# The conditioning projection in four column tiles of TensorE, spread over attention and the dense feed-forward

## The reference, cut to what matters

```python
def _modulation(cvec, w, b):
    return (jax.nn.silu(cvec) @ w + b)[:, None, :]

def _layer(x, mod, p, cache, ffn):
    sh1, sc1, g1, sh2, sc2, g2 = jnp.split(mod, 6, axis=-1)
    y, ctx_state = _token_mixers(_rmsnorm(x, p['norm1']) * (1 + sc1) + sh1, p, cache)
    x = x + g1 * y
    x = x + g2 * ffn(_rmsnorm(x, p['norm2']) * (1 + sc2) + sh2)
```

## Time and profile before

| | us |
|---|---|
| Median of 3 runs (2623.82 to 2625.38) | 2624.83 |
| The profiled execution's own time | 2626.07 |
| Its span | 2624.3 |
| TensorE busy | 2336.5 (89%) |
| VectorE busy | 1585.4 (60%) |
| ScalarE busy | 1094.0 (42%) |
| Mean granted TensorE clock | 0.924 of full |

### The profile page before, as it was taken

The page is one execution under the profiler, slowest core; times in us unless marked ns, Lnnn a source line. Parts: engine busy times, 40 slices in busy tenths (PEclk is TensorE's granted clock), DMA queues, the critical chain, the costliest instruction groups (busy, mean ns, idle before and its releaser), DMA issues.

```text
span 2624.3 us, 52068 instructions
## 1 busy us (share of the span) xinstructions
PE 2336.5 (89%) x22774; PEld 1463.2 (56%) x22774; DVE 1585.4 (60%) x2462; ACT 1094.0 (42%) x1398; POOL 71.5 (3%) x70
## 2 busy tenths in 40 slices
PE   7799998869789999999899998868787999998894
PEld 4366667856445555555456668855563444444442
DVE  0364645549554545533174654549638999997886
ACT  0223342226432222221132342235526888886774
POOL 0000000000000000000000000000001111110001
PEclk9889988978889999999989997988878999999997
DMA  9621100010122212214821101010009999998995
GB/s 337 209 73 50 34 29 15 4 68 1 65 81 81 81 65 97 81 49 139 278 73 50 34 1 43 4 68 1 1 19 368 402 409 407 408 408 343 360 355 223
DMA packets 58290, 381.23 MB, mean 145 GB/s; under 512 B 7280, under 2 KB 8432, under 8 KB 16592
## 3 DMA queue, kind: packets, MB, share of 16 engines
q1 hardware_dynamic: 50160, 346.18, 34.5%
q0 software_dynamic: 7904, 31.72, 3.2%
HBM read 362.41 MB, written 15.47 MB: 144 GB/s over the span
## 4 chain that ended last, share of the span: by engine, by line
PE 38%; DVE 7%; ACT 3%; DVEq 1%; DMA 1%; issue 1%; ACTq 0%; POOL 0%; PEldq 0%
PE ps L1870 7%; PE ps L1844 4%; PE ps L1845 4%; PE ps L1846 4%; PE ps L147 3%; PE ps L148 3%; PE ps L149 3%; PE ps L1160 1%; DVE att L1467 1%; PE ps L1156 1%; PE ps L1144 1%; PE ps L1765 1%; PE ps L1626 1%; PE ps L1854 1%; PE ps L825 0%
## 5 line engine op out<-in xcount | busy, mean ns | idle before, releaser
L147 PE MATMUL ps<-scan,work 128*128 128x512 f16 (+1 forms) x1024 | 290.4, 307 | 38.2 <-DVE work L256 22.5
L148 PE MATMUL ps<-scan,work 128*128 128x512 f16 (+1 forms) x1024 | 291.6, 307 | 0.0
L149 PE MATMUL ps<-scan,work 128*128 128x512 f16 (+1 forms) x1024 | 288.0, 307 | 0.0
L303 PE MATMUL ps<-ring,work 128*48 128x256 f32 x768 | 172.5, 389 | 19.4 <-DMA ring<-in_wmod 15.2
L249 ACT ACTIVATE work<-ring 128x2048 f16<-128x2048 f32 x52 | 98.4, 1903 | 170.2 <-DVEq L185 89.1
L1828 DVE SCALAR_TENSOR_TENSOR work<-ring,work 128x2048 f16<-128x2048 f32 x68 | 154.1, 2287 | 21.4 <-ACT work L1824 21.4
L147 PEld LDWEIGHTS ps<-scan,work 128*128 128x128 f16 x1024 | 101.4, 99 | 116.6 <-issue 41.7
L147 PE MATMUL ps<-pj,scan 128*128 128x128 f16 (+1 forms) x544 | 150.9, 301 | 15.3 <-DVE pj L410 8.4
L1828 DVE SCALAR_TENSOR_TENSOR scan<-ring,scan 128x2048 f16<-128x2048 f32 x68 | 155.5, 2287 | 8.4 <-ACT scan L1824 8.4
L1828 DVE SCALAR_TENSOR_TENSOR pj<-hT,pj 128x2048 f16<-128x2048 f32 x68 | 152.5, 2284 | 6.2 <-ACT pj L1824 6.2
L256 DVE SCALAR_TENSOR_TENSOR work<-ring,work 128x2048 f16<-128x2048 f32 x52 | 118.5, 2288 | 60.4 <-ACT work L249 60.1
(11 more groups left out here) (406 smaller groups left out, 5225.1 us busy)
## 6 DMA issues: line engine op xcount, KB each, us to landing
ring<-in_e SPq DMA_DIRECT2D x136, 1024.0 KB, 8.5
hT<-in_e SPq DMA_DIRECT2D x68, 1024.0 KB, 7.9
ring<-in_wmod SPq DMA_DIRECT2D x48, 1024.0 KB, 4.9
ring<-in_d SPq DMA_DIRECT2D x33, 1024.0 KB, 4.9
ring<-in_win SPq DMA_DIRECT2D x24, 1024.0 KB, 4.9
yslots<-pj POOLq DMA_DIRECT2D x17, 512.0 KB, 8.5
ring<-in_wout SPq DMA_DIRECT2D x8, 1024.0 KB, 8.4
ring<-in_wv SPq DMA_DIRECT2D x4, 1024.0 KB, 4.9
```

Of the source, the lines that this page charges most:

```text
L147: nc.tensor.matmul(out, w[0], x[0], start=start, stop=False)
L148: nc.tensor.matmul(out, w[0], x[1], start=False, stop=False)
L149: return nc.tensor.matmul(out, w[1], x[0], start=False, stop=stop)
L303: mm = nc.tensor.matmul(ps[0:MROW, 0:WCOL], padded[:, k, PAD - 2 * j:PAD - 2 * j + MROW], w[:, k, :], start=(j == 0 and k == 0), stop=(j = ...
```

## The change

A group is now four tiles of `w_mod`, which fill the array side by side. The array is used as four tiles of 128 rows x 32 columns. The stationary operand `cpad` has 32 columns for each block, the two vectors and 30 of zeros. Matmul t of a group writes partitions 32t to 32t+31. So the four weight tiles are multiplied in turn, k by k, each in its own column tile, and all four are given free at the end. Six groups make a layer; a group is one of the six vectors.

- Layer 0: groups 0 and 1 (shift and scale of the first norm) run at the start. Only they are loaded ahead of the input projection's tiles. Groups 2 to 5 come through the ring after the scans, ahead of the output projection's tiles. Each runs just before the scores of pairs 4, 7, 10 and 13, and VectorE copies its rows out inside `logits_dve`. After attention their rows are turned and added (`mod_late_pe`, `mod_late_dve`).
- Layer 1: GpSimd loads the groups into `pj` and `hT`, which lie idle then, a group at a time, after the second norm of layer 0. Group g runs ahead of the down products of item g+1. At item 8 the rows are turned and added into `mod_next`. At the end of the feed-forward they are copied to `mod` (`mod_turn_dve`).
- Both first norms: the first tile of the input projection of layer 0 is split inside the norm's loop (before ScalarE's block 4, before VectorE's step 5). The barriers of the modulation stages are gone.

```diff
@@ -186,14 +186,18 @@
             eng.wait_ge(meeting, 3 * met[who])
-        base_mod = [0, 0]
+        MGROUP = 4
         base_in, base_out, base_ffn = [0, 0], [0, 0], [0, 0]
         n = 0
+        base_late = 0
         for l in range(DEPTH):
-            base_mod[l] = n
-            n += N_MOD
+            if l == 0:
+                n += 2 * MGROUP
             base_in[l] = n
             n += N_IN + 2
+            if l == 0:
+                base_late = n
+                n += N_MOD - 2 * MGROUP
             base_out[l] = n
             n += N_OUT
             base_ffn[l] = n
@@ -289,57 +293,132 @@
...
+        N_GROUP = N_MOD // MGROUP
+        cpad = wk[:, 4800:4800 + KT * 32].rearrange("p (k c) -> p k c", k=KT)
+        vt = vtok[:, :, :].rearrange("p a b -> p (a b)")
+        pick = ident[:, :].rearrange("p (t c) -> p t c", t=4)[:, :, 0:2]
+        mod_next = vt[:, 1536:1632].rearrange("p (m s) -> p m s", s=2)
+        mflat = (pj[:, 0:8, :].rearrange("p a b -> p (a b)"), hT[:, :, :].rearrange("p a b -> p (a b)"))
+        def mrow(l, g):
+            return wk[:, 3200 + WCOL * (g - 2):3200 + WCOL * (g - 1)] if l == 0 and g >= 2 else vt[:, WCOL * g:WCOL * g + WCOL]
+        def mbuf(t):
+            return mflat[t // 2][:, SLOT * (t % 2):SLOT * (t % 2) + SLOT]
+        def pad_dve(dve):
+            nc.vector.memset(cpad, 0.0)
+            dve.drain()
+            nc.vector.tensor_copy(cpad[:, :, 0:2], cT[:, :, :])
+            dve.drain().then_inc(S["c_padded"], 1)
+        def mod_group_pe(out, srcs, used):
+            for k in range(KT):
+                for t in range(MGROUP):
+                    mm = nc.tensor.matmul(out[32 * t:32 * t + 32, :], cpad[:, k, :], srcs[t][:, k, :],
+                                          start=(k == 0), stop=(k == KT - 1))
+                    if k == KT - 1:
+                        mm.then_inc(used, 1)
+        def mod_ring_pe(pe, n, out):
+            for t in range(MGROUP):
+                pe.wait_ge(w_loaded[(n + t) % NSLOT], 16 * uses(n + t))
+            mod_group_pe(out, [slot3(n + t) for t in range(MGROUP)], w_used)
+        def mod_cols_pe(l, g, out):
             for m in range(2):
+                mm = nc.tensor.matmul(out[:, 8 * m:8 * m + 8].rearrange("p (t s) -> p t s", s=2),
+                                      mrow(l, g)[:, m * P:(m + 1) * P], pick, start=True, stop=True)
+            return mm
+        def mod_add_dve(l, g, dst, src):
             for m in range(2):
+                ins = nc.vector.tensor_tensor(dst[:, 8 * g + m:8 * g + 8:2, :],
+                                              src[:, 8 * m:8 * m + 8].rearrange("p (t s) -> p t s", s=2),
+                                              par[:, l, C_BMOD + 8 * g + m:C_BMOD + 8 * g + 8:2].unsqueeze(2).to_broadcast([P, 4, 2]),
+                                              ALU.add)
+            return ins
+        def mod_end_dve(dve, l, groups):
+            dve.drain()
+            for g in groups:
+                m = mod[:, 8 * g:8 * g + 8, :]
+                if g in (2, 5):
+                    nc.vector.tensor_scalar(m, m, 1.0 / W_SCALE, None, ALU.mult)
+                if g in (1, 4):
+                    c = C_N1 if g == 1 else C_N2
+                    nc.vector.scalar_tensor_tensor(s1[:, g // 4], m, 1.0, par[:, l, c:c + 8].unsqueeze(2).to_broadcast([P, 8, 2]),
+                                                   ALU.add, ALU.mult)
+            dve.drain()
+        def mod_first_pe(pe):
+            pe.wait_ge(S["c_padded"], 1)
+            for g in range(2):
+                mod_ring_pe(pe, MGROUP * g, bank(2 + g)[:, 0:WCOL])
+                if g == 0:
+                    norm_pe(pe, 0)
+            for g in range(2):
+                pe.wait_ge(S["mod_row"], g + 1)
+                mod_cols_pe(0, g, bank(4 + g)[:, 0:16]).then_inc(S["mod_cols"], 1)
+        def mod_first_dve(dve):
+            for g in range(2):
+                dve.wait_ge(w_used, MGROUP * (g + 1))
+                nc.vector.tensor_copy(mrow(0, g), bank(2 + g)[:, 0:WCOL]).then_inc(S["mod_row"], 1)
+                if g == 0:
+                    dve.wait_ge(consts_loaded, 16 * N_CONST)
+                    for k in range(KT):
+                        square_sum_dve(dve, 0, k)
+            for g in range(2):
+                dve.wait_ge(S["mod_cols"], g + 1)
+                mod_add_dve(0, g, mod, bank(4 + g)[:, 0:16])
+            mod_end_dve(dve, 0, (0, 1))
+        LATE_AT = {4: 2, 7: 3, 10: 4, 13: 5}
+        def mod_late_pe(pe):
+            pe.wait_ge(S["mod_row"], N_GROUP)
+            for g in range(2, N_GROUP):
+                mm = mod_cols_pe(0, g, bank(6)[:, 16 * g:16 * g + 16])
+            mm.then_inc(S["mod_cols"], 1)
+        def mod_late_dve(dve):
+            dve.wait_ge(S["mod_cols"], 3)
+            for g in range(2, N_GROUP):
+                mod_add_dve(0, g, mod, bank(6)[:, 16 * g:16 * g + 16])
+            mod_end_dve(dve, 0, range(2, N_GROUP))
+            dve.drain().then_inc(S["mod_done"], 1)
+        def mod_next_pe(pe, item, at):
+            g = item - 1
+            if 0 <= g < N_GROUP:
+                pe.wait_ge(S["m1_loaded"], 64 * (g + 1))
+                mod_group_pe(at[:, 256:512], [mbuf(t).rearrange("p (k c) -> p k c", k=KT) for t in range(MGROUP)], S["m1_used"])
+            if item == 8:
+                pe.wait_ge(S["mod_row"], 2 * N_GROUP)
+                for g in range(N_GROUP):
+                    mod_cols_pe(1, g, at[:, 256 + 16 * g:272 + 16 * g])
+        def mod_next_dve(dve, item, at):
+            g = item - 1
+            if 0 <= g < N_GROUP:
+                nc.vector.tensor_copy(mrow(1, g), at[:, 256:512]).then_inc(S["mod_row"], 1)
+            if item == 8:
+                for g in range(N_GROUP):
+                    mod_add_dve(1, g, mod_next, at[:, 256 + 16 * g:272 + 16 * g])
+        def mod_turn_dve(dve):
+            dve.drain()
+            nc.vector.tensor_copy(mod[:, :, :], mod_next)
+            mod_end_dve(dve, 1, range(N_GROUP))
         rstd = wk[:, 2 * SLOT:2 * SLOT + T]
...
@@ -383,6 +462,9 @@
+                if k == 4:
+                    for phase, n in within_it:
+                        split_hi(act, phase, n)
@@ -399,6 +481,9 @@
+                if k == 5:
+                    for phase, n in within_it:
+                        split_lo(dve, phase, n)
@@ -1389,6 +1474,8 @@
+            if l == 0 and i in LATE_AT:
+                mod_ring_pe(pe, base_late + MGROUP * (LATE_AT[i] - 2), bank(2)[:, 256:512])
@@ -1454,6 +1543,8 @@
+            if l == 0 and i in LATE_AT:
+                nc.vector.tensor_copy(mrow(0, LATE_AT[i]), bank(2)[:, 256:512]).then_inc(S["mod_row"], 1)
@@ -2014,6 +2109,8 @@
             for d in range(KT):
                 q = q0 + d
                 pe.wait_ge(S["f_free"], q - 3)
+                if d == 0:
+                    mod_next_pe(pe, item, bank(2 * (q % 4) + 1))
                 for a, e in PIECES:
                     for c in range(2):
                         mm = mm3(pair(q)[:, a:e], [x[:, c, d * P:(d + 1) * P] for x in w],
@@ -2145,20 +2244,24 @@
             for dst, name in ((par, "par"), (cT, "cT")):
                 sp.dma_start(dst[:], A[name]).then_inc(c_loaded, 16)
             for j in range(NSLOT):
-                load(base_mod[0] + j, A["wmod"][0, j])
+                load(j, A["wmod"][0, j])
             consts = [(ident, "ident"), (ones, "ones"), (blk, "blk"), (rot, "rot"), (sel, "sel"),
                       (cmask, "cmask"), (incl, "incl"), (lvl, "lvl"), (swamask, "swamask"), (nmask, "nmask"),
                       (wup, "wup"), (rt, "router"), (tri, "tri"), (before, "before"), (tokid, "tokid"), (xT, "xT")]
             for dst, name in consts:
                 sp.dma_start(dst[:], A[name]).then_inc(consts_loaded, 16)
             for l in range(DEPTH):
-                for j in range(NSLOT if l == 0 else 0, N_MOD):
-                    load(base_mod[l] + j, A["wmod"][l, j])
+                if l == 0:
+                    for j in range(NSLOT, 2 * MGROUP):
+                        load(j, A["wmod"][0, j])
                 for j in range(N_IN):
                     load(base_in[l] + j, A["win"][l, j])
                 for j in range(2):
                     load(base_in[l] + N_IN + j, A["wv"][l, j])
                 sp.wait_ge(S["mixer_d_done"], l + 1)
+                if l == 0:
+                    for j in range(N_MOD - 2 * MGROUP):
+                        load(base_late + j, A["wmod"][0, 2 * MGROUP + j])
                 for j in range(N_OUT):
                     load(base_out[l] + j, A["wout"][l, j])
                 b = base_ffn[l]
@@ -2194,6 +2297,13 @@
                 pool.dma_start(A["new_v"][l], vtok[:, 0, :]).then_inc(S["states_out"], 16)
                 pool.wait_ge(S["mixer_d_done"], l + 1)
                 pool.dma_start(A["new_std"][l], st_d[0][:]).then_inc(S["states_out"], 16)
+                if l == 0:
+                    pool.wait_ge(S["hk_ready"], 2 * KT)
```

(28 more changed lines are left out.)

71 lines of the change are left out of this document (19 added, 52 removed).

## The result

The changed kernel takes 2501.47 us, the median of 4 runs (2496.23 to 2502.59), against 2625.11 us before (4 runs, 2623.82 to 2626.73): ratio 0.9525, 95% interval 0.9508 to 0.9541. The forecast was 2511 us in 2497 to 2536. The profiled execution of after took 2496.23 us, span 2494.4, 129.9 less than the span before; it is the lowest of the four.

A forecast was written before the change was run, and what follows sets the result against it. TensorE, not the weights, was taken to set the modulation's pace. The terms -69 - 89 + 17 + 2 + 25.5 gave -113.5 against the profiled 2626.1 us: 2512.6, as a median 2511 us, range 2497 to 2536.

The forecast's parts named there:

- G: Price on TensorE of one modulation group in four column tiles: 3.8 us, with a two-tile bound of 7.7 us.
- Start of layer 0: Modulation and norm ahead of layer 0's input projection: -69 us (-63 to -73), VectorE's loop starting at 45.9 us.
- Start of layer 1: Tiles, copies and barriers ahead of layer 1's norm loop go: -89 us (-87 to -90).
- Attention: Four groups ahead of scores in layer 0's attention make VectorE wait, 3.6 us each: +17 us (+10 to +24).
- They just fit: In attention, a next group's weight tiles take 12 us to load, against 14.5 us for three pairs.
- Before the output norm: Between attention and out_pe, additions and mod operations sit ahead of VectorE's split: +2 us.
- Feed-forward: Layer 0's feed-forward, TensorE taken as full: six groups 22.8 us plus columns 2.7 us, +25.5 us (+22 to +34).
- The columns' own price: Feed-forward item 8: 12 matmuls of 8 columns, 24 records at 0.11 us, 2.7 us, at most 5.2.
- lowest and highest sums: Whole kernel with all low bounds together 2491 us, with all high ones 2543 us, called unlikely at once.
- only two tiles overlap: Rival for the modulation groups: only two column tiles run together, a group takes 8.0 us, +47, 2558 us; chance 0.09.
- Late weights: Rival in attention: each of three groups waits 6 us for weights, +18, 2529 us; chance 0.07.
- Tiles one after another: Rival for the modulation groups: column tiles don't overlap, 14.0 us a group, 2628 us, no change, or 2663; chance 0.02.

The follow-up runs named there:

- the repeat: The changed kernel as it is, run once more beside the other runs of this chip: 2501.76 us (2496.93 to 2502.39).

## Why the prediction held, and where its sum was off

- **G.** 3.8 us was taken from two tiles that overlap and one tile's stream. Measured: 3.59 from the first record to the next product, 3.65 as a row, at full clock; four records come every 0.215 us, one tile's own pace. The lower bound was the right one to take. The prediction's 0.060 us for two tiles has the longer first step of its row in it. The second row gives 0.055: its eight records start at 619.68 and the next row at 620.12. So two tiles already reached 2 of 2. The change of tiling was put at 0.17 us each way; 3.59 less 16 x 0.216 leaves 0.13 for both. The Trainium skill, TensorE: Matmul & The Clock Gate, section "Measured speedup vs the span model", gives 3.07 times for four row tiles (of 512 columns); an estimate by it, with the 0.3 us for the change of tiling, is 4.8 us. The trace doesn't agree: 13.7 / 3.59 is 3.8 times.
- **Start of layer 0**: -70.4 for -69. The loop starts 72.8 us earlier, for 71.5, and is 2.4 longer, for 2.5. Group 1, feared cold at 4.8, took 3.89 here, and 4.14 to 5.5 in other executions; in those of the kernels with the same start (the repeat, the groups at layer 1's start, in the up products, doubled, at every fourth pair) the second split stands 0.2 to 1.5 us later than here. So the better end of the range is in part luck.
- **Start of layer 1**: -89.3 for -89.
- **Attention**: +17.6 for +17, and the nearness is partly luck. Seven profiles of kernels with this attention lie between +15.6 and +20.8. The two groups at full clock, at pairs 10 and 13, put VectorE a further 4.0 and 3.5 us behind the kernel before, for 3.6. "They just fit" was false at the first pairs: the next four tiles came 13.7 us after the group before (530.08 to 543.75), for the predicted 12, and there was work for 10.6 of them (3.07 us of wait and 1.7 for the clock). On the other side the group at pair 4 took 4.65, for 5.5, and at the end of attention the kernel before ran at a granted clock of 0.58 (678 to 682 us), the changed one at 1.00 (620 to 625), which gives 1.6 us back.
- **Before the output norm**: +2.0 for +2.
- **Feed-forward: the term that was mis-sized.** The prediction says "TensorE is the bound: 26.00 of 26 us, nothing idle", so "everything put there counts in full", +25.5. It measured +16.8: six items at 2.31 and the columns' item at 2.95 more. The window that it rests on the earlier trace rows is called one item, but it is 26 us of an item of 40.5, and TensorE's wait for VectorE's residual stands just ahead of it:

```profile
826.83 0.39 PE L147 MATMUL ps<-pj,scan 128*128 128x512 f16 x1 [1.21 <-DVE xT L1551]
```

A window over one whole item of the kernel before shows what the 26 us hid:

```profile
816.00:856.50 40.50, 39.29 (x290) 22.11 (x288) 20.15 (x28) 10.52 (x9) 0.00 (x0) 1.00 0.21 78
```

TensorE is busy for 39.29 of 40.50, and the table of waits over the stage shows the 1.2 us nine times. The columns' own price was right, 24 records in 2.80 us for 2.7. Their item came out near it for another reason: the wait covers 1.2 of it, and the fall of the clock behind them, which other profiles lack, adds 1.4 to 1.7.
- **The rest.** The profile fell by 129.9 for the predicted 113.5. Of the 16.4 between, 8.7 are the feed-forward, 1.4 the start of layer 0, 4.8 the unchanged stretch and 1.8 what lies behind the start of layer 1; the other terms cancel. The medians fell by only 123.6, since the profiled execution is 5.2 below its median and that of the kernel before 1.0 above. That the 3.3 us of the clock are absent from the six higher executions fits their times, but they have no trace. The prediction's lowest and highest sums (2491 and 2543) are not worked out there: the terms' bounds, as written, add up to 2496 and 2535.

Of the rivals, that only two tiles overlap was made into a kernel (25 us slower than the changed one, for the 47 predicted), but it is not this one. Late weights came at one group, for 4.8 us and not 18. Tiles one after another did not reach "no change": ten groups of 11.4 in place of 14.0 us are 26 us less than the rival's 2628, and the kernel ended 27 us below the one before the change.

## What to carry to other kernels

A matmul with few stationary columns was worth column tiles here even in fp32, but only with successive instructions on different tiles: write the loop over tiles innermost. Before calling a stage full, read its table of waits over whole periods, not a window inside one. Work that was put exactly where the bottleneck engine waits was cheaper by that wait, and where the wait was longer than the work (ahead of the first scores) it cost nothing that the rows show. Groups that are moved need their weights' transfer time between them, cold starts included: a 3 us wait cost nearly 5. And before a stage's change is read to a tenth of a microsecond, look at how far the same code's stage moves between profiles; here attention moved by 5 us.

## What was not expected of the hardware

- Two column tiles overlap fully (64 records of 256 columns in 6.21 us) and four fully (3.59 us), in fp32, with moving operands from two different buffers.
- Without interleaving, records of one tile come every 0.216 us. But at a change of tile the next tile's first four records run beside the last four of the one before, so that a group takes 11.43 us and not 13.7.
- The same code's stretch of 250 us comes in two lengths in the profiles, 244.5 to 245.7 us (four profiles) and 248.9 to 249.0 (eight), by GpSimd's idle time; one of each kind has granted clocks of 0.97 and 0.91 in its last 50 us.
- 24 records of 8 columns, put into a stretch of dense products, were followed by a fall of the clock to 1.2 GHz in six of eleven profiles; without the fall the stage was 1.4 to 1.7 us shorter.
